# Query blocks of two expert layers as 512-column products of high and low tokens

## The reference

```python
def peer_ffn(h, wq, keys, u, v):
    q = (h @ wq).reshape(B, S, PEER_HEADS, 2, half)      # h: 256 x 1024, wq: 1024 x 2048
    s1 = jnp.einsum('bshd,hnd->bshn', q[..., 0, :], keys[:, 0])
    s2 = jnp.einsum('bshd,hnd->bshn', q[..., 1, :], keys[:, 1])
    v1, i1 = lax.top_k(s1, 16)
    v2, i2 = lax.top_k(s2, 16)
    ...                                  # 16 experts of each of 8 heads are chosen, gates are a softmax
    act = gelu(einsum('td,ted->te', ht, u[et]))
    return einsum('te,ted->td', gt * act, v[et])
```

## Time and profile before

| what | value |
|---|---|
| time, three runs | 2275.99, 2277.54 (median), 2280.52 us |
| the profiled execution | 2274.92 us, its span 2273.1 us |
| PE busy | 2242.3 us, 99% |
| DVE, ACT busy | 1743.5 us (77%), 1323.0 us (58%) |
| mean granted TensorE clock | 0.998 of 2.4 GHz |
| query blocks | about 143 to 198 us and 1073 to 1128 us |

### The profile page before, as it was taken

The page is one execution under the profiler, slowest core; times in us unless marked ns, Lnnn a source line. Parts: engine busy times, 40 slices in busy tenths (PEclk is TensorE's granted clock), DMA queues, the critical chain, the costliest instruction groups (busy, mean ns, idle before and its releaser), DMA issues.

```text
span 2273.1 us, 36462 instructions
## 1 busy us (share of the span) xinstructions
PE 2242.3 (99%) x13873; PEld 1964.5 (86%) x13873; DVE 1743.5 (77%) x3559; ACT 1323.0 (58%) x2400; POOL 586.3 (26%) x411
## 2 busy tenths in 40 slices
PE   8999999999999999999999999999999999999999
PEld 8889888888787878888988888888888878899998
DVE  7966999899787878667499998976666666747864
ACT  6765665665545554566566666555554455676643
POOL 4820388774000000011017887700000000003000
PEclk9999999999999999999999999999999999999999
DMA  7724577776788888665257777766666665324441
GB/s 275 254 96 146 187 191 185 173 169 168 267 295 282 292 285 292 256 213 202 93 183 193 190 176 171 169 215 223 216 220 217 216 242 205 130 112 176 185 192 61
DMA packets 168790, 455.24 MB, mean 200 GB/s; under 512 B 44885, under 2 KB 80285, under 8 KB 160681
## 3 DMA queue, kind: packets, MB, share of 16 engines
q1 hardware_dynamic: 135024, 452.40, 58.5%
q0 software_dynamic: 33280, 0.15, 4.1%
q10 hardware_dynamic: 312, 0.37, 0.1%
HBM read 432.76 MB, written 20.09 MB: 199 GB/s over the span
## 4 chain that ended last, share of the span: by engine, by line
PE 85%; DVE 9%; ACT 3%; DMA 2%; issue 1%; ACTq 0%; DVEq 0%
PE PS L174 85%; DVE r_sl L195 3%; DMA mem<-in_v 2%; DVE mem L195 2%; ACT r_sh L185 1%; DVE mem L203 1%; ACT mem L185 1%; DVE mem L209 1%; PE PS L177 0%; DVE hT L203 0%; ACT small L185 0%; DVE mem L215 0%; DMA mem<-in_ada 0%; DMA cst<-in_cst 0%; DVE r_gl L203 0%
## 5 line engine op out<-in xcount | busy, mean ns | idle before, releaser
L195 DVE TENSOR_TENSOR r_sl<-mem,r_sh 128x1024 fp32r<-128x1024 f32 (+2 forms) x750 | 896.3, 1196 | 375.6 <-ACT r_sh L185 374.3
L185 ACT ACTIVATE r_sh<-mem 128x1024 fp32r<-128x1024 f32 (+2 forms) x750 | 768.0, 1025 | 492.5 <-PE PS L174 394.7
L174 PE MATMUL PS<-r_h,r_sh 128*128 128x512 f32 (+2 forms) x3536 | 736.4, 350 | 8.9 <-ACT r_sh L185 4.0
L174 PEld LDWEIGHTS PS<-r_h,r_sh 128*128 128x128 f32 (+1 forms) x3536 | 559.7, 189 | 86.1 <-issue 8.5
L235 POOL DMA_INDIRECT gd<-mem x224 | 407.6, 1820 | 120.1 <-issue 77.5
L174 PEld LDWEIGHTS PS<-r_h,r_sl 128*128 128x128 f32 (+1 forms) x2832 | 381.0, 191 | 23.4 <-DVE r_sl L195 3.6
L174 PE MATMUL PS<-r_h,r_sl 128*128 128x256 f32 (+1 forms) x2832 | 399.7, 283 | 1.2 <-DVE r_sl L195 1.1
L174 PE MATMUL PS<-r_sh,r_ch 128*128 128x512 f32 x1024 | 277.1, 391 | 4.5 <-ACT r_sh L185 2.3
L174 PE MATMUL PS<-r_sh,r_cl 128*128 128x512 f32 x1024 | 274.8, 389 | 0.0
L174 PE MATMUL PS<-r_sl,r_ch 128*128 128x512 f32 x1024 | 274.7, 389 | 0.0
L174 PEld LDWEIGHTS PS<-r_sh,r_ch 128*128 128x128 f32 x1024 | 190.6, 188 | 51.7 <-ACT r_sh L185 7.5
(11 more groups left out here) (177 smaller groups left out, 2548.1 us busy)
## 6 DMA issues: line engine op xcount, KB each, us to landing
mem<-in_u SPq DMA_DIRECT2D x256, 512.0 KB, 3.9
mem<-in_v SPq DMA_DIRECT2D x256, 512.0 KB, 4.4
mem<-in_w SPq DMA_DIRECT2D x16, 2048.0 KB, 7.7
mem<-in_ada SPq DMA_DIRECT2D x48, 512.0 KB, 5.3
mem<-in_in SPq DMA_DIRECT2D x9, 2048.0 KB, 8.8
gd<-cst SPq DMA_DIRECT2D x16, 1024.0 KB, 9.8
mem<-in_wq SPq DMA_DIRECT2D x8, 2048.0 KB, 8.9
r_h<-gd SPq DMA_DIRECT2D x62, 256.0 KB, 4.8
```

What stands on the lines that cost most here:

```text
L174: return self.did(self.e and self.e.matmul(out, lhsT, rhs, start=start, stop=stop, skip_group_check=skip))
L185: return self.did(self.e and self.e.activation(out, in_, func, **kw))
L195: return self.did(self.e and self.e.tensor_tensor(out, a, b, op))
```

## The change

Blocks 1 to 15 of the query product go from `mm_T` to `mm_pairs`. The gained tokens' high and low parts become one tensor `r_g`, so that both can be one moving operand of 512 columns. The two halves of the bank have to be added. ScalarE now copies the right half to one of two buffers `q_half` (event `qhalf`), and VectorE adds the left half to it and writes the query (new function `query`). Query 0, which still fills only 256 columns, is copied by VectorE in place of ScalarE. VectorE's turn i gets `query(i - 1)` directly behind `lo` of block i + 1, and `query(15)` stands behind the loop.

```diff
--- before.py
+++ after.py
@@ -106,7 +106,7 @@
 
 TOLD_ON = {}
 for _sem, _events in (
-        ("gla_ac", "uhalf bf softplus lexp decay kdrow meanS ysq varL rstd o osq oln orr silu_r"),
+        ("gla_ac", "uhalf qhalf bf softplus lexp decay kdrow meanS ysq varL rstd o osq oln orr silu_r"),
         ("gla_ve", "usum cumsum ldiff dd level qd kd centred normed yb"),
         ("gla_pe", "gate lmm kdT kv mean var gla oss"),
         ("cmp_ac", "cmpS kc_sq kc_ln kc_r Lexp PcT"),
@@ -331,12 +331,14 @@
 
     H = nc.alloc_sbuf_tensor_at("r_h", [128, 4096], F32R, offset=hT_at)
     hlo, hhi = H[:, 0:2048], H[:, 2048:4096]
+    G = nc.alloc_sbuf_tensor_at("r_g", [128, 4096], F32R, offset=mem_at + 4 * A)
+    g_pairs = G[:, :].rearrange("p (w x) -> p w x", w=2)
     h_pairs = H[:, :].rearrange("p (w x) -> p w x", w=2)
     hhi_raw_r = hhi.bitcast(F32)
-    GH, GL = in_f32r("gh", 0, 2048), in_f32r("gl", 2048, 2048)
+    GH, GL = G[:, 0:2048], G[:, 2048:4096]
     SH, SL = ([in_f32r(f"s{w}{i}", AR + 2048 * i + 1024 * (w == "l"), 1024) for i in range(2)] for w in "hl")
     hhiv, hlov = chunks(hhi[:, :], 8), chunks(hlo[:, :], 8)
-    ghiv, glov = chunks(GH[:, :], 8), chunks(GL[:, :], 8)
+    ghiv, glov = chunks(GH, 8), chunks(GL, 8)
     xT, hT = chunks(xTf[:, :], 8), chunks(hTf[:, :], 8)
 
     def C(name, rows=128):
@@ -1267,6 +1269,7 @@
     ecode = ecand.bitcast(U32)
     cand2 = [take(NP + 2)[:, 0:NP] for _ in range(2)]
     hot = take(16 * NP)
+    q_half = [hot[:, 0:256], hot[:, 256:512]]
     v16 = take(256).rearrange("p (h k) -> p h k", h=8)
     i16 = take(256).bitcast(U32).rearrange("p (h k) -> p h k", h=8)
     f16 = take(256).rearrange("p (h k) -> p h k", h=8)
@@ -1422,10 +1425,11 @@
                 p, j = i // 4, i % 4
                 if i + 1 < len(qs) and i > 1:
                     hi(ac, n + 1)
-                ac.wait_ge("wdone", n)
-                if p >= 2:
-                    ac.wait_ge("scored", layer, p - 2, 1)
-                ac.activation(qTb[p % 2][:, j, :], PS[:, (i + 1) % 4, 0:256], COPY).then_inc("q", layer, p, j)
+                if i:
+                    ac.wait_ge("wdone", n)
+                    if i > 2:
+                        ac.wait_ge("q", layer, (i - 2) // 4, (i - 2) % 4)
+                    ac.activation(q_half[i % 2], PS[:, (i + 1) % 4, 256:512], COPY).then_inc("qhalf", layer, i)
                 if i == 0:
                     hi(ac, n + 2)
                     ac.ready(LNEXP)
@@ -1647,9 +1651,23 @@
 
         COST = 2 * (16 * 15 + 8 * 13 + 8 * 20) + 3 * (6 + 28 + 20)
 
+        def query(ve, i):
+            p, j, b = i // 4, i % 4, (i + 1) % 4
+            if p >= 2:
+                ve.wait_ge("scored", layer, p - 2, 1)
+            q = qTb[p % 2][:, j, :]
+            if i:
+                ve.wait_ge("qhalf", layer, i)
+                ve.tensor_tensor(q, PS[:, b, 0:256], q_half[i % 2], ADD).then_inc("q", layer, p, j)
+            else:
+                ve.wait_ge("wdone", WQ[0][0])
+                ve.tensor_copy(q, PS[:, b, 0:256]).then_inc("q", layer, p, j)
+
         def peer_ve(ve):
             for i, n in enumerate(n for p in WQ for n in p):
                 lo(ve, n + 1)
+                if i:
+                    query(ve, i - 1)
                 if 2 <= i < 8:
                     c = OWN[i - 2]
                     ve.wait_ge("rr", k)
@@ -1658,6 +1676,7 @@
                     c = OWN[i - 3]
                     ve.wait_ge("hhi", k, c)
                     ve.tensor_tensor(hlov[:, c, :], hT[:, c, :], hhiv[:, c, :].bitcast(F32), SUB).then_inc("hlo", k, c)
+            query(ve, 15)
             pick, spent = choices(ve), 0
 
             def gate_low():
@@ -1818,7 +1837,7 @@
                     gained_block(pe, n, 1, (ghiv, glov), k, ("q", layer, 0, 0), ())
                 else:
                     bank_wait(pe, (i + 1) % 4)
-                    mm_T(pe, n, PS[:, (i + 1) % 4, 0:256], (ghiv, glov), between=(lambda: square_total(pe, k, hT)) if i == 1 else None)
+                    mm_pairs(pe, n, (i + 1) % 4, g_pairs, ghiv, between=(lambda: square_total(pe, k, hT)) if i == 1 else None)
                     emptied[(i + 1) % 4] = ("q", layer, i // 4, i % 4)
                 if i == 2:
                     turn_scale(pe, k, 7)
```

## The result

| | median | lowest to highest | runs |
|---|---|---|---|
| before | 2276.47 us | 2274.08 to 2280.52 | 16 |
| after | 2282.95 us | 2280.73 to 2287.22 | 16 |

The ratio is 1.0029, with a 95% interval of 1.0021 to 1.0037, so +6.5 us (+4.8 to +8.4). The profiled execution after has a span of 2281.1 us, against 2273.1.

What follows compares the result with a forecast made beforehand. TensorE, busy 99% of the span, was taken as the bound. 2 x (1.9 loop + 2.4 tail - 1.3 saving) + 1.4 clock = 7.4 us on the 2277.54 median gave 2284.9 us, 0.3% slower; range 2280.0 to 2289.5.

Steps and rivals of the forecast that it cites:

- TensorE's saving: Query blocks 1 to 15 take 2.79 us instead of 2.88, saving 1.3 us a layer, 2.6 in both.
- The loop: ScalarE-VectorE cycle in query blocks 2 to 7 slows from 3.06 to 3.40 us; TensorE waits cost 1.9 us a layer.
- The rival of a saving near nothing: Wide products on TensorE save nearly nothing; worked with no saving, +10.0 us, 2287.5; chance 0.03.
- The second rival (slack holds): Additions fall into VectorE's waits, so only the tail costs: +2.2 us, 2279.7, within 0.2%; chance 0.12.
- The tail: Last scores wait 3.0 us for queries 14 and 15, added behind the first expert block's low part; 2.4 us a layer.
- Sum without the clock: Over both layers, loop plus tail less TensorE's saving, 2 x (1.9 + 2.4 - 1.3): 6.0 us slower.
- The clock: TensorE's clock may halve behind the tail's wait: 0 to 5.4 us for both layers, 1.4 taken; full-fall rival +11.4, chance 0.2.

Runs made afterwards that it cites:

- fifth run: The kernel before with only the 512-column products in blocks 1 to 15, right half left out of the queries, no VectorE additions: 2275.72 us, ratio 0.9990.
- second run: The changed kernel with the addition moved to the end of VectorE's turn, queries 14 and 15 left in place: 2279.66 us, ratio 1.0017 against the kernel before.
- tenth: The kernel before with one more 256-column VectorE addition, result unused, behind the low part in each query-block turn: 2282.42 us against 2279.29, ratio 1.0021.
- first run: The changed kernel with the additions of queries 14 and 15 ahead of the first expert block's low part: 2275.64 us, ratio 0.9999 against the kernel before.
- the sixth: The kernel before with only the copies of queries 14 and 15 moved to VectorE, behind the first expert block's low part: 2284.10 us, ratio 1.0031.
- the two kernels with the fill: The changed kernel with ten or twelve idle 512-column products in each layer's wait: 2283.24 us both, ratios 1.0031 and 1.0024 against the kernel before.
- its second timing: The changed kernel unaltered, timed again beside the fill of twelve products: 2287.25 us, ratio 1.0041 against the kernel before.

## Why the prediction was right, point by point

- **TensorE's saving**, forecast 2 x 1.3 us: blocks at 2.79, and the fifth run, -2.3 us. The rival of a saving near nothing is out, as far as an interval that ends at 1.0000 can say.
- **The loop**, forecast 3.40 us a turn and 1.9 us a layer, before blocks 6, 7 and 9: found 3.38 to 3.39, at those blocks, 1.6 us. TensorE had 0.3 us more in hand at block 4 than I had put (the block starts at 157.76, its conversion ends at 156.79: 0.97, where I had 156.12 and 155.45). Shown both ways: putting the addition elsewhere brings back 3.06 (second run), adding one to the old kernel makes the waits (tenth). The second rival (slack holds) is out.
- **The tail**, forecast a wait of 3.0 us and 2.4 us of cost a layer: found 2.5 in layer 1. Shown both ways too, by the first run and the sixth.
- **Sum without the clock**, forecast 6.0: 2 x (1.6 + 2.5 - 1.3) = 5.6. Layer 1, where the clock stayed, went by itself from 1128.54 - 1073.27 = 55.27 us (block 0 to the first expert block) to 1136.51 - 1078.45 = 58.06, +2.8. The two starts of block 0 are in these rows of before and of after:

```profile
1073.27 0.34 PE L174 MATMUL PS<-r_gh,r_sh 128*128 128x256 f32 x1
```
```profile
1078.45 1.77 PE L174 MATMUL PS<-r_g,r_sh 128*128 128x256 f32 x13
```

- **The clock**, forecast 0 to 5.4 us, 1.4 taken: a fall costs 1.5 us (layer 0 after), little more than half of the 2.7 that I had as its upper bound, since it is over sooner than the one of the earlier trace rows. It occurs more often than I took it. The four kernels that have the wait unfilled (the change twice, the second run, the sixth) have eight such places in their traces, and behind six of them the clock was lowered; in the two kernels with the fill, behind none of four. Six in eight at 1.5 us would be 2.3 us an execution, an estimate. The times agree with it in size only: above their sums without the clock (5.6, 5.6, 2.5 and 5.2 us) the change stands 0.9 us, its second timing 3.7, the second run 1.4 and the sixth 1.9, each give or take 2 to 3 us. The forecast of 7.4 and the measured 6.5 both lie in the interval of 4.8 to 8.4, so how much of it is the clock stays open.
- **How close it came, and luck in it.** 2284.9 was forecast and 2282.95 measured. Of the 2.0 us between, 1.1 is the base: I forecast from the median of three runs, 2277.54, and that of sixteen is 2276.47. The rest is small errors that partly cancel: the loop 0.6 too much for both layers, the tail 0.2 too little, the clock perhaps 0.9 too little. The mechanism is what was right; the closeness of the sum is in part luck.

## What to carry to other kernels

A saving on the engine that bounds is worth its face value only if what it needs stays early, and for that the place of an operation in its engine's list counts more than its duration: 0.42 us additions on an engine idle for 23% of the time cost 1.6 us a layer in one place, 2.5 in another, and next to nothing in a third. Before an operation moves to another engine, look in that engine's list for what stands ahead of it and what that waits for, above all at the turn from one stage to the next, where the steady pattern ends. And measure a wait from start to start: the trace's idle time began some 0.2 to 0.5 us too late here.

## What the runs showed that I had not expected

The clock falls behind short waits as well, and in some executions only. Near 131 us, before anything that the change touches, TensorE has waits of 0.56, 0.56 and 0.30 us, in before and after alike to 0.01 us. First after, three rows, then the first of them in before:

```profile
125.22 0.39 PE L174 MATMUL PS<-r_h,r_sh 128*128 128x256 f32 x1 [0.56 <-ACT mem L185]
128.91 0.39 PE L174 MATMUL PS<-r_h,r_sh 128*128 128x256 f32 x1 [0.56 <-ACT r_sh L185]
129.70 0.38 PE L174 MATMUL PS<-r_h,r_sh 128*128 128x256 f32 x1 [0.30 <-ACT r_h L185]
```
```profile
124.71 0.39 PE L174 MATMUL PS<-r_h,r_sh 128*128 128x256 f32 x1 [0.56 <-ACT mem L185]
```

The stretch behind them, after (columns as in the earlier trace rows), and TensorE's first products of block 0:

```profile
130.97:134.38 3.41, 3.41 (x14) 3.19 (x15) 2.46 (x5) 1.52 (x4) 0.00 (x0) 0.50 0.00 0
```
```profile
144.27 1.71 PE L174 MATMUL PS<-r_g,r_sh 128*128 128x256 f32 x13
```

The clock was 0.50 there in this profiled execution, and was not lowered at that place in that of before. Of the twelve traces of this study five have it, always for 3.4 us. Block 0 started 1.6 us later after (144.27 against 142.66) without the change having a part in it. Of this 0.5 was there ahead of the stretch (125.22 against 124.71), and the other 1.1 is the clock: from that row to block 0 it takes 17.95 to 17.97 us in the seven traces without the fall and 19.04 to 19.22 in the five with it. So a fall cost 1.1 to 1.3 us here. This is also some of the 8.0 us between the two spans, of which only 6.5 are the medians' difference. Two single traces of this kernel are not compared to better than a few microseconds; stretches within them are.
